# Loading rows before a modulation cut in column halves, and expert scatters that add into two places per token

## What is computed

```
mod = silu(c) @ w_ada + b_ada                     # (1024 x 6144), per sequence
shift1, scale1, gate1, shift2, scale2, gate2 = split(mod, 6)
h = rmsnorm(x, g_mix) * (1 + scale1) + shift1
q, k, v, b, c, u, gate_a, gate_b = split(h @ w_in)  # 46 column tiles of 128
... attention, short convolution, merge ...
x = x + gate1 * (merged @ w_o)
h = rmsnorm(x, g_ffn) * (1 + scale2) + shift2
y = sum over the top 2 experts of a token of  weight * (silu(h Wg) * (h Wu)) Wd   # 32 experts
out = rmsnorm(x + gate2 * y, g_final)
```

## Time and profile before

| | |
|---|---|
| median of 3 runs | 789.85 us (789.43 to 791.33) |
| profiled execution, own time | 789.53 us |
| its span, first to last instruction | 787.8 us |
| mean granted TensorE clock | 0.947 |
| busy: PE, PEld, DVE, ACT, POOL | 694.5, 532.7, 318.0, 165.7, 123.9 us |
| moved by DMA | 198.48 MB, 252 GB/s over the span |

### The profile page before, as it was taken

One profiled execution on the slowest core, in us unless ns is written; L12 is line 12 of the kernel. 1 busy time (PEld: TensorE's weight loads), 2 busy tenths in 40 slices (PEclk: granted clock), 3 DMA queues, 4 the chain that ended last, 5 costly groups with the idle time before them and its releaser, 6 DMA issues.

```text
span 787.8 us, 12170 instructions
## 1 busy us (share of the span) xinstructions
PE 694.5 (88%) x5003; PEld 532.7 (68%) x5003; DVE 318.0 (40%) x701; ACT 165.7 (21%) x323; POOL 123.9 (16%) x189
## 2 busy tenths in 40 slices
PE   2589999999999999999999999779999988788820
PEld 1289989879899889999997455555565554455500
DVE  2162232135688773322234765425232322211235
ACT  4062222221154442112110111111111111100001
POOL 2400000410006001000000100123333332222112
PEclk9989999999999999999999999769999999988975
DMA  9843546856143438421105972779999999999873
GB/s 293 331 160 140 215 174 267 324 215 222 54 133 118 151 105 331 169 69 67 55 27 177 415 294 87 255 291 400 415 414 413 411 413 417 416 414 416 356 302 151
DMA packets 40399, 198.48 MB, mean 252 GB/s; under 512 B 8174, under 2 KB 8358, under 8 KB 24720
## 3 DMA queue, kind: packets, MB, share of 16 engines
q1 hardware_dynamic: 31088, 175.42, 57.3%
q0 software_dynamic: 8352, 21.81, 8.0%
q10 hardware_dynamic: 904, 0.47, 0.3%
HBM read 188.54 MB, written 17.40 MB: 261 GB/s over the span
## 4 chain that ended last, share of the span: by engine, by line
PE 81%; DMA 6%; DVE 4%; issue 4%; ACT 2%; SPq 1%; POOL 1%; POOLq 0%; DVEq 0%
PE bank L1632 31%; PE bank L1878 16%; PE bank L1833 7%; PE bank L1900 7%; DMA arena<-in_w_in 5%; PE bank L1776 4%; PE bank L1871 2%; PE bank L1773 2%; PE bank L1570 2%; PE bank L1668 2%; PE bank L1731 1%; PE bank L1794 1%; PE bank L1895 1%; DMA arena<-y_scratch 1%; PE bank L1714 1%
## 5 line engine op out<-in xcount | busy, mean ns | idle before, releaser
L1632 PE MATMUL bank<-h_parts,w_parts 128*128 128x260 f32 x2160 | 273.4, 286 | 0.8 <-DVE w_parts L1068 0.6
L1632 PEld LDWEIGHTS bank<-h_parts,w_parts 128*128 128x128 f32 x2160 | 263.8, 189 | 9.9 <-issue 8.2
L1878 PE MATMUL bank<-arena,arena_b 128*64 128x256 f32 x704 | 89.8, 412 | 13.5 <-issue 9.1
L1068 DVE TENSOR_TENSOR w_parts<-arena,w_parts 128x1024 fp32r<-128x1024 f32 x46 | 56.2, 1222 | 71.3 <-ACT w_parts L897 71.1
L1878 PEld LDWEIGHTS bank<-arena,arena_b 128*64 128x64 f32 x704 | 57.6, 148 | 39.5 <-issue 12.3
L1422 DVE TENSOR_TENSOR arena_b<-bank,arena_b 128x128 f32<-128x128 f32 x32 | 9.3, 292 | 129.8 <-ACT arena_b L1000 129.7
L897 ACT ACTIVATE w_parts<-arena 128x1024 fp32r<-128x1024 f32 x46 | 48.4, 1052 | 55.9 <-DMA arena<-in_w_in 41.9
L829 POOL DMA_INDIRECT y_scratch<-arena_b x32 | 33.2, 1037 | 161.9 <-DVE arena_b L1447 154.4
L1833 PE MATMUL bank<-arena,arena_b 128*128 128x512 f32 x128 | 56.7, 597 | 0.0
L1878 PE MATMUL bank<-arena_b 128*64 128x256 f32 x320 | 40.1, 407 | 6.1 <-issue 5.3
L1900 PE MATMUL bank<-arena,arena_b 128*64 128x512 f32 x176 | 42.3, 593 | 0.8 <-DVE arena_b L1428 0.8
(11 more groups left out here) (301 smaller groups left out, 761.1 us busy)
## 6 DMA issues: line engine op xcount, KB each, us to landing
arena<-in_w_gate_up SPq DMA_DIRECT2D x44, 1024.0 KB, 29.1
arena<-in_w_in SPq DMA_DIRECT2D x46, 512.0 KB, 4.9
arena<-in_w_ada SPq DMA_DIRECT2D x22, 1024.0 KB, 7.2
arena<-in_w_down SPq DMA_DIRECT2D x20, 1024.0 KB
arena_b<-in_w_gate_up SPq DMA_DIRECT2D x20, 1024.0 KB
arena_b<-in_w_down SPq DMA_DIRECT2D x20, 512.0 KB
arena_b<-in_x_prompt SPq DMA_DIRECT2D x8, 512.0 KB, 7.8
arena_b<-q_scratch POOLq DMA_DIRECT2D x3, 1024.0 KB, 5.7
```

The lines of the kernel that those rows point to most:

```text
L1068: dve.tensor_tensor(w_parts[:, n % 2, 1], ring[:, n % WRING], w_parts[:, n % 2, 0], ALU.subtract).then_inc(s_wlo, 1)
L1632: ins = pe.matmul(ps[s][:, 0:HALF], w_parts[:, n % 2, wp, k], h_parts[:, hp, k, s * HALF:(s + 1) * HALF], start=(k == 0 and hp == 1), stop ...
L1878: ins = pe.matmul(ps[2 + b][R * hh:R * hh + R, 0:2 * P], hTe[:, b, c * P + jj * R:c * P + jj * R + R], w_gu[slot][jj][:, c, :, hh * P:(hh ...
```

## The change

**At the beginning.** SP loads the x rows first, then group 0's weights in two halves of 4 MB, with the tiles 0 and 1 between them. A half holds columns 0 to 511 (then 512 to 1023) of both shift1 and scale1, all a feature block k of 0 to 3 (4 to 7) needs; the host lays each half's four steps out as contiguous 1 MB blocks (`w_ada0`). In a half's step the two feature rows go to different partition quarters, and a product with a sum of identity quarters (`both_quarters`, 64 columns) transposes and adds them (`turn_mods`). Scale, shift and the two-part rows of k = 0 to 3 are made after the first half, those of 4 to 7 after the second. Tiles 0 and 1 of the projection are both run block by block (`tile_step`), in banks of their own, and both weight splits stand among the blocks. The biases of groups 1 and 2 are loaded by ACT between k = 3 and k = 4.

**At the end.** x is written to place 0 of the token (`y4[.., 0]`) and zeros to place 1 (a DMA of 2 MB issued by POOL during attention), and each scatter adds into its rows (`compute_op=ALU.add`). The reload of x is gone, and DVE forms place 0 plus place 1 in one addition per block; the samples' normalisation stands last. Semaphores that can share one (`s_neg`, `s_own`, `s_exp2`) do; no wait differs by that.

```
-            for a in range(4):
-                load_ada(a)
-                if a == 0:
-                    for i in range(5):
-                        sp.dma_start(x[0:rows[i], i], xp_v[i] if i < 4 else xs_v).then_inc(s_x[i], 16)
-            load_tile(0)
+            for i in range(5):
+                sp.dma_start(x[0:rows[i], i], xp_v[i] if i < 4 else xs_v).then_inc(s_x[i], 16)
+            load_first(0)
+            for n in range(WRING):
+                load_tile(n)
+            load_first(1)
...
-                    sp.dma_start(x_d[i * P:i * P + P], x[:, i]).then_inc(s_xw, 16)
+                    sp.dma_start(y4[i * P:i * P + P, 0], x[:, i]).then_inc(s_xw, 16)
...
-            for i in range(4):
-                sp.dma_start(x[:, i], x_d[i * P:i * P + P]).then_inc(s_xl, 16)
...
+            link(pool.memset(x[:, 4], 0.0))
+            pool.dma_start(y4[0:TP, 1].rearrange("(i p) d -> p i d", p=P),
+                           x[:, 4].unsqueeze(1).to_broadcast([P, 4, D])).then_inc(s_zero, 16)
...
                 pool.indirect_dma_start(out=y_d, out_offset=bass.IndirectOffsetOnAxis(ap=ix, axis=0),
-                                        in_=ys[:, j % YB], in_offset=None, bounds_check=last_written, oob_is_err=False
-                                        ).then_inc(s_sc[j], 16)
+                                        in_=ys[:, j % YB], in_offset=None, bounds_check=last_written, oob_is_err=False,
+                                        compute_op=ALU.add).then_inc(s_sc[j], 16)
...
+            def first_step(half, s):
+                if half == 0:
+                    pe.wait_ge(s_ada[s], 16)
+                else:
+                    pe.wait_ge(s_adb[s // 3], 16 if s == 3 else 48)
...
+                for kk in range(2):
+                    for jj in range(2):
+                        q = 32 * (2 * jj + kk)
+                        ins = pe.matmul(ps[6][q:q + 32, :], cvec[:, 2 * s + kk], ada0[half][s][:, kk, jj],
+                                        start=(s == 0), stop=(s == 3), skip_group_check=True)
+                ins.then_inc(s_adamm, 1)
...
+            def summed(i, c=slice(0, D)):
+                dve.wait_ge(s_yk[i], 16)
+                dve.tensor_tensor(x[:, i, c], yk[:, i, 0, c], yk[:, i, 1, c], ALU.add).then_inc(s_x2, 1)
```

More of the change, by code:

```diff
@@ L170, in hybrid_step @@
         wo = [cube(arena[:, wo0_at:wo0_at + 4 * D], KD), cube(region("SPLIT", 0, 4 * D), KD)]
[L171 to L174, removed]
+        ada0 = [[region("SPLIT", (4 + 2 * s) * D, 2 * D) for s in range(4)],
+                [region(("CACHE", "QK")[s // 2], 2 * (s % 2) * D, 2 * D) for s in range(4)]]
+        ada0 = [[r.rearrange("p (k j n) -> p k j n", k=2, j=2) for r in half] for half in ada0]
+        ada = cube(region("CACHE", 0, 4 * D), 2)
         qT = cube(region("QK", 0, AT * T), AT)
@@ L333, in hybrid_step @@
         s_ada = [sem(f"s_ada{i}") for i in range(4)]
-        s_ada_end = sem("s_ada_end")
+        s_adb = [sem(f"s_adb{i}") for i in range(2)]
         s_bada = sem("s_bada")
@@ L507, in hybrid_step, with h_done @@
         y4 = y_d.rearrange("(t k j) d -> t k (j d)", k=2, j=2)
+        tile_bank = [(ps[3], ps[7]) if n == 1 else (ps[0], ps[1]) for n in range(len(ORDER))]
+        row_bank = [(ps[2 + 2 * (n % 2)], ps[3 + 2 * (n % 2)] if n else ps[6]) for n in range(NQKV)]
+        def h_done(k):
+            return k + 2 if k < 4 else k + 3
         def at_least(eng, s, v):
@@ L1116, in by_rows @@
                 dve.tensor_copy(dst, sm[0:TS, 0:P]).then_inc(s_tok, 1)
-            for n in range(NQKV):
+            for n in range(1, NQKV):
                 split(n + 1)
-                if n:
-                    by_rows(n - 1)
+                by_rows(n - 1)
                 if n in (9, 17):
@@ L1575, in turn_x, with turn_mods @@
+            def turn_mods(half):
+                pe.wait_ge(s_adaev, half + 1)
+                for cc in range(4):
+                    ins = pe.matmul((ps[0], ps[6])[half][:, 64 * cc:64 * cc + 64], mods[:, cc], both_quarters,
+                                    start=True, stop=True, skip_group_check=True)
+                ins.then_inc(s_modT, 1)
             def turn_x(k):
-                at_least(pe, s_hA, k - 3)
+                at_least(pe, s_hA, 5 if k == 7 else k - 3)
                 for i in range(NB):
-                    ins = pe.transpose(ps[TURNED[k % 4]][:, i * P:(i + 1) * P], x[:, i, k * P:(k + 1) * P], idn)
+                    ins = pe.transpose(ps[TURNED[k]][:, i * P:(i + 1) * P], x[:, i, k * P:(k + 1) * P], idn)
@@ L1579, in turn_x, with tile_step @@
                 ins.then_inc(s_xT, 1)
-            for a in range(2):
-                ada_step(a)
+            def tile_step(n, k):
+                if k == 0:
+                    pe.wait_ge(s_whi, n + 1)
+                    pe.wait_ge(s_wlo, n + 1)
+                pe.wait_ge(s_hA, k + 1)
+                pe.wait_ge(s_hD, h_done(k))
+                for s in range(2):
+                    for wp, hp in ((0, 1), (0, 0), (1, 0)):
+                        ins = pe.matmul(tile_bank[n][s][:, 0:HALF], w_parts[:, n, wp, k],
+                                        h_parts[:, hp, k, s * HALF:(s + 1) * HALF],
+                                        start=(k == 0 and hp == 1), stop=(k == KD - 1 and wp == 1),
+                                        skip_group_check=True)
+                    if k == KD - 1:
+                        ins.then_inc(s_half, 1)
@@ L1583, in _ @@
+            for s in range(4):
+                first_step(0, s)
             pe.wait_ge(s_xn, 5)
@@ L1989, in laid_out @@
         out[name] = cached(t[name], s)
-    out |= {name: t[name] for name in ("cache_conv", "c_prompt", "c_sample", "g_mix", "w_ada", "b_ada")}
+    out |= {name: t[name] for name in ("cache_conv", "c_prompt", "c_sample", "g_mix")}
+    first = t["w_ada"][0][:, 0:2 * D].reshape(4, 2, P, 2, 2, 512)
+    out["w_ada0"] = first.transpose(4, 0, 2, 1, 3, 5).reshape(2, 4, P, 2 * D)
+    out["w_ada"] = t["w_ada"][:, :, 2 * D:]
+    out["b_ada"] = t["b_ada"]
     out["w_in"] = w_in[[n for _, n, _ in ORDER]]
```

284 lines of the change are left out of this document (145 added, 139 removed).

## The result

The change makes the kernel slower: median 798.75 us of 3 runs (796.96 to 799.07) against 789.85, ratio 1.0111 with a 95% interval of 1.0095 to 1.0128. The profiled execution took 798.75 us, its span is 796.9, 9.1 longer than before. I had forecast 786.8, a gain of 2.7, in a range up to 797.0: the measured time lies above the range.

What follows compares the result with a forecast made beforehand. PE's chain was taken to bound most of the kernel, the full DMA queues the expert stage; 789.5 - 4.8 (start) - 3.2 (end) + 5.3 (scatters) = 786.8 us, range 780.0 to 797.0.

Steps and rivals of the forecast that it cites:

- The first half comes after the same 6 MB: Start: the first half of group 0's weights is in at 23.4 us, the first modulation stands at 27.6.
- PE still owes (the order above): Start: list of PE's remaining blocks and steps, bytes in at 35.9 us, ending at 40.3; second modulation at 42.0.
- Shared semaphores cost nothing: no wait moves: Whole kernel: letting semaphores share one was claimed to cost 0, since no wait moves.
- In the change PE is busier ahead of them, so I keep the higher level: Start: PE's higher clock was assumed for the second half's products, in the sum giving a gain of 4.8 us.
- My lower bound: Start: with PE at the lower clock, the second half's 48 products cost 6.0 us more, leaving minus 1.2.
- The upper bound: Start: if the second modulation waits only for its data (35.9), tile 2 starts near 49.1, a gain of 8.2 us.
- the nearest row is half a gather: Expert stage: an adding scatter's extra read priced at 0.177 us, a cost of 5.3 us for 30 scatters.
- The upper end of 0.354: Expert stage: upper price per scatter if the added read doubles it, 10.6 us for 30 scatters.
- the read counts in full: Expert stage rival: the added read costs 10.6 us, total 792.6, queue share near 15%, last weights 5.8 later; chance 0.24.
- The stall: Expert stage rival: engines stall on each read before the write, 0.7 us a scatter, 21 more, total 802.5; chance 0.09.
- The end: After the last scatter: fewer additions end the kernel at 778.6 against 781.93, gain 3.2 us, at most 4.9, at least 2.
- The zeros: Attention, 310 to 315 us: the 2 MB of zeros cost nothing while PE covers them, at most 5 us.

Runs made afterwards that it cites:

- e3: The changed kernel with a semaphore of its own for each of the four chunks of the second half of group 0's weights; 792.47 us, ratio 1.0042.
- e6: The change's start with a semaphore per chunk and PE's order changed, with the old end of the kernel before; 781.07 us, ratio 0.9888.
- e8: The kernel before with one more indirect gather for each of experts 9 to 31, into a region nobody reads; 802.99 us, ratio 1.0162.
- e4: The changed kernel with scatters that write without adding, so the output leaves out x; 785.97 us, ratio 0.9957.
- e2: The kernel before with only the change's end, so the old start stays; 797.38 us, ratio 1.0105.
- e1: The changed kernel with the end of the kernel before, so only the start is changed; 791.74 us, ratio 1.0027.
- e5: The change's start with a semaphore for each chunk, with the end of the kernel before; 787.37 us, ratio 0.9958.
- e9: The change's start with a semaphore per chunk and PE's order changed, with the change's adding end; 788.06 us, ratio 0.9989.
- e10: Old end and shared semaphore kept, all four steps of the second half put behind tile 0's first four blocks in PE's order; 783.91 us, ratio 0.9926.

## Why the prediction was wrong

Of the 12.0 us between 786.8 and 798.75, 7.6 are the start (a gain of 4.8 forecast, 2.8 lost), 4.9 the scatters and -0.4 the end; the rest, -0.1, lies between the stages.

- **First half**: in at 20.94, not 23.4, the modulation applied from 24.45, not 27.6. "The first half comes after the same 6 MB" missed that the same bytes come faster, at 338 GB/s in the first slice against 293. Whether the new order of loads or the new layout does it, no run separates. This was in the change's favour.
- **The step that failed at the start** is "PE still owes (the order above)". I listed the steps' work and the end of their bytes, 35.9, but gave the first of them no wait of its own, though the order shows it ahead of all of tile 0's blocks and the diff shows it waiting for three chunks. From this one line come the stand of 5.63 us, the clock of 0.50 after it and the second modulation at 47.20 instead of 42.0. e3 takes the wait away and has the modulation at 39.87. The 35.9 itself was right: e6's last step waits for its bytes until 35.67. "Shared semaphores cost nothing: no wait moves" overlooked this one. The list also leaves out tile 1's fourth block, which stands ahead of the transpose; in the trace it runs beside the bias and costs nothing.
- **"In the change PE is busier ahead of them, so I keep the higher level"** failed too, and not because of the three chunks alone. PE was busy for all of 37 to 45 us at 0.98, but then stood for 2.74 us around the second modulation, a gap that my own sum has (from the last step at 40.3 to block 4 at 44.1, with little for PE between), and the second half's products ran at 0.62 in 50 to 54 us. e3, without the first wait, shows the same stand and 0.50 in 42 to 46. e6 covers the stand with ready blocks down to 0.54 us, and the clock stays at 1.00. My lower bound for this, minus 1.2, was passed by 1.0 (tile 2 at 59.54 against 57.34), since the wait and the clock came together. The upper bound, tile 2 near 49.1, is what e6 reaches, 49.10, but with another order of PE, which the bound didn't have.
- **The scatters**: the term was mis-sized. I took 5.3, measured are 10.2 in the change and 9.7 to 11.4 in the six pairs that differ in the addition, 0.32 to 0.38 each. The choice "the nearest row is half a gather" was the error. Halving a queue's share assumed that a gather's read and write each cost half; e8 gives 0.43 for a whole gather (0.32 by its share), and the addition costs nearly that. The upper end of 0.354 was the better value, and the rival "the read counts in full" had the price and the queue share (near 15%, measured 15.0%). The last weights came 12.95 later; it said 5.8, the start's 4.8 gain included, which here was a loss of 2.8.
- The Trainium skill, "Collectives: The Full Stack", section on the bandwidth ceiling, says of a collective's reduce step that its addition is slow because it takes two source reads on one ring. The trace agrees in kind: with additions POOL's queue rose from 9.9% to 15.0%, and with half of them to 12.9%.
- **The stall** didn't come: of its 0.7 us per scatter the runs show at most 0.39, and half the additions cost about half.
- **The end**: forecast -3.2, measured -3.6. The closeness is luck: the sum left the last scatter's landing as it was, and it came 1.4 later (only its "at least 2" allowed for that), while what follows the landing shrank by 5.0, over the stated maximum of 4.9. e4, where the landing stays at 2.35, has -4.6. My sum put the root of block 0 behind the addition of block 1; in the trace it runs beside that addition and DVE doesn't wait for it, and from that addition (779.57) to DVE's last operation it is 11.4 us, where I had 12.7.
- **The range**: its upper end was called full reads with a poor start, but my own rows for these, 792.6 and the start at minus 1.2 instead of 4.8, give 798.6. Stopping at 797.0 had no row behind it.
- **The zeros**: right. The share of 310 to 315 us rose from 0.52 to 0.98, and PE was busy for all 5.00 us, as before. In e2, with the old start and the zeros, the first gather comes at 515.84, not later than the 516.39 before.

```profile
310.00:315.00 5.00, 5.00 (x38) 4.82 (x38) 0.56 (x1) 0.78 (x2) 0.00 (x0) 1.00 0.98 338
```

With the start (2.8 by the first gather), the scatters and the end as measured, the sum gives 789.5 + 2.8 + 10.2 - 3.6 = 798.9 against 798.75. That is bookkeeping of the same trace; what confirms the terms is that e3 takes the wait away, e4 the additions, and that start and end come back apart in e1 and e2.

## What to carry to other kernels

Before crediting a gain to an earlier start, walk the in-order engine's list and write beside every entry what its wait counts up to; a wait for several transfers at once, standing ahead of work that is ready, undid the gain here, and the clock that fell after it made it a loss. Look for the gaps that your own sum leaves in TensorE, too, and put ready work into them (e6: 0.54 us of standing instead of 2.74). In a stage whose queues are full, price an adding scatter as a scatter with a whole gather beside it, and set the saving that it brings at the end (here 3.6 us) against that times its number (here 30). And when two executions are compared late in a program, first subtract what they already differ by at the stage's entry: without that, half the additions would be priced at 6.2 us instead of 4.3.

## What the runs showed that I had not expected

- An adding scatter holds POOL longer at its issue, 1.61 us against 1.04 in the mean. The page's groups, before and after:

```profile
L829 POOL DMA_INDIRECT y_scratch<-arena_b x32 | 33.2, 1037 | 161.9 <-DVE arena_b L1447 154.4
```

```profile
L835 POOL DMA_INDIRECT y_scratch<-arena_b x32 | 51.5, 1608 | 154.0 <-DVE arena_b L1476 133.1
```

- The addition appears as packets of POOL's queue (778 more in 100 us for 14 scatters, 56 each) but not as its megabytes: that queue's bytes alone would have shown no cost.
- The products of the first half run at two paces in different executions with the same granted clock of 1.00: eight took 1.06 us in e3 and 1.94 in e5 at 20.84. In e5 the slower pace lasts until about 29 us, and its second modulation is 2.2 us later (42.04 against 39.87), tile 2 1.3 later. e9 and e10 ran at the slower pace too (1.93 and 1.83), e6 at the faster one (1.06), so differences of about 1 us between these beginnings may be this and not the edit. Why the pace changes stays open.

```profile
20.84 1.94 PE L1611 MATMUL bank<-arena,arena_b 128*32 128x512 f32 x8 [0.56 <-DMA arena<-in_w_ada]
```
